# RWKV block inverse: the products Q of levels 1 to 4 as 32x32 tiles taken straight from the scores, without GpSimd's masked copy

## The reference

```python
    def step(S, inp):
        r_t, w_t, k_t, v_t, kk_t, a_t = inp
        sa = -jnp.einsum('dbhvk,dbhk->dbhv', S, kk_t)
        S = (S * w_t[..., None, :] + sa[..., :, None] * (kk_t * a_t)[..., None, :]
             + v_t[..., :, None] * k_t[..., None, :])
        return S, jnp.einsum('dbhvk,dbhk->dbhv', S, r_t)
```

## Time and profile before

| what | value |
|---|---|
| median of 3 runs | 2774.28 us (2770.97 to 2775.0) |
| the profiled execution's own time | 2774.59 us |
| its span in the profile | 2772.8 us |
| PE busy over the span | 2613.4 us, 94% |
| PEld busy | 2134.0 us, 77% |
| DVE busy | 1935.2 us, 70% |
| ACT busy | 1178.1 us, 42% |
| POOL busy | 295.0 us, 11% |
| granted clock of PE, mean | 0.979 of full |
| instructions fetched: queue q8 | 113 packets, 1.85 MB |

### The profile page before, as it was taken

How to read it: one execution, slowest core, us unless ns; L and a number is a source line. 1 busy time by engine, 2 the same in 40 slices (tenths; PEclk the granted TensorE clock), 3 DMA queues, 4 the chain that set the end, 5 groups by cost and what they waited for, 6 DMA issues and landing times. The chain is left out here.

```text
span 2772.8 us, 42554 instructions
## 1 busy us (share of the span) xinstructions
PE 2613.4 (94%) x17846; PEld 2134.0 (77%) x17846; DVE 1935.2 (70%) x1901; ACT 1178.1 (42%) x1390; POOL 295.0 (11%) x240
## 2 busy tenths in 40 slices
PE   3999978998999999999999799999999999999996
PEld 3888857776777888888888687888778888888885
DVE  5788856666576888888887878865668755555557
ACT  2555544445443333333333345555443333333332
POOL 0000001111004000000000094641040000000000
PEclk9999989998999999999999899999999999999998
DMA  8899734331548888888887366754468755555552
GB/s 310 313 330 348 288 135 132 107 126 62 213 153 297 326 304 319 310 308 322 309 320 288 116 233 241 260 167 168 155 240 324 251 187 191 190 188 193 186 195 78
DMA packets 259418, 636.55 MB, mean 230 GB/s; under 512 B 10606, under 2 KB 17444, under 8 KB 239300
## 3 DMA queue, kind: packets, MB, share of 16 engines
q1 hardware_dynamic: 253106, 621.68, 63.1%
q10 hardware_dynamic: 6162, 12.72, 1.2%
HBM read 632.25 MB, written 2.10 MB: 229 GB/s over the span
## 5 line engine op out<-in xcount | busy, mean ns | idle before, releaser
L534 DVE TENSOR_TENSOR s_wl<-s_raw,s_wh 128x2048 fp32r<-128x2048 f32 (+1 forms) x393 | 913.7, 2325 | 519.0 <-ACT s_wh L529 510.0
L529 ACT ACTIVATE s_wh<-s_raw 128x2048 fp32r<-128x2048 f32 x396 | 758.4, 1916 | 1085.2 <-PE pa L739 417.3
L737 PE MATMUL pa<-s_wh,s_hth 128*128 128x512 f32 x1312 | 527.1, 402 | 14.3 <-DVE s_wl L534 9.1
L738 PE MATMUL pa<-s_wl,s_hth 128*128 128x512 f32 x1312 | 516.9, 394 | 0.0
L739 PE MATMUL pa<-s_wh,s_htl 128*128 128x512 f32 x1312 | 516.4, 394 | 0.0
L737 PEld LDWEIGHTS pa<-s_wh,s_hth 128*128 128x128 f32 x1312 | 249.7, 190 | 76.6 <-DVE s_wl L534 13.2
L739 PEld LDWEIGHTS pa<-s_wh,s_htl 128*128 128x128 f32 x1312 | 249.8, 190 | 53.9
L738 PEld LDWEIGHTS pa<-s_wl,s_hth 128*128 128x128 f32 x1312 | 250.0, 191 | 48.8
L737 PE MATMUL pb<-s_wh,s_hth 128*128 128x512 f32 x704 | 274.1, 389 | 0.0
L738 PE MATMUL pb<-s_wl,s_hth 128*128 128x512 f32 x704 | 273.9, 389 | 0.0
L739 PE MATMUL pb<-s_wh,s_htl 128*128 128x512 f32 x704 | 273.9, 389 | 0.0
(11 more groups left out here) (406 smaller groups left out, 3446.0 us busy)
## 6 DMA issues: line engine op xcount, KB each, us to landing
s_raw<-in_ffn_w_in SPq DMA_DIRECT2D x176, 1024.0 KB, 5.3
s_adaw<-in_ada_w SPq DMA_DIRECT2D x144, 1024.0 KB, 5.4
s_raw<-in_ffn_w_out SPq DMA_DIRECT2D x88, 1024.0 KB, 7.6
s_raw<-in_ab_w_in SPq DMA_DIRECT2D x48, 1024.0 KB, 9.2
s_raw<-in_diff_w_in SPq DMA_DIRECT2D x48, 1024.0 KB, 5.2
s_adaw<-in_ada_w SPq DMA_DIRECT2D x48, 512.0 KB, 6.0
s_raw<-in_ab_w_out SPq DMA_DIRECT2D x16, 1024.0 KB, 5.2
s_qkv<-in_ada_w SPq DMA_DIRECT2D x16, 1024.0 KB, 7.2
```

Source lines behind the costliest of these rows:

```text
L529: act.activation(wh[:, s % 2, :, 0:width], raw[:, s, :, 0:width], ACT.Copy).then_inc(hi_done, 1)
L534: dve.tensor_tensor(wl[:, s % 2, :, 0:width], raw[:, s, :, 0:width], wh[:, s % 2, :, 0:width].bitcast(F32), ALU.subtract).then_inc(lo_done, 1)
L737: pe.matmul(o, a_hi, w_hi, start=start and k == 0, stop=False)
L738: pe.matmul(o, a_hi, w_lo, start=False, stop=False)
```

## The change

`level_q` takes its weights from `R_GA` itself, four 32x32 tiles a unit, as `level_v` does. `R_D`, the mask `own_block`, its 64 columns of constants, `diagonal` and the semaphore `diag_ready` are gone, with the waits on it.

```diff
-        R_D = sb("R_D", [P, NU, CH], stack=r2)
@@ POOL @@
             def own_w(t):
-                pool.wait_ge(diag_ready, t + 1)
                 pool.wait_ge(wt_ready, 4 * t + 4)
...
-            def diagonal(n):
-                pool.wait_ge(g_ready, 4 * n + 2)
-                if n:
-                    pool.wait_ge(own_ready, n)
-                    pool.wait_ge(q_done, 5 * n - 1)
-                pool.tensor_tensor(R_D[:], R_GA[:, n % 3, :, 0:CH], own_block.unsqueeze(1).to_broadcast((P, NU, CH)),
-                                   ALU.mult).then_inc(diag_ready, 1)
...
-                if t + 1 < PAIRS:
-                    diagonal(t + 1)
@@ PE, level_q @@
                     pe.wait_ge(first_ready, t + 1)
-                    pe.wait_ge(diag_ready, t + 1)
                     pe.wait_ge(wf_ready, t)
...
                 for u in range(NU):
-                    mm = two(quarter(L1Q, u), R_D[:, u], R_V[:, u], start=(u == 0))
+                    for g in range(4):
+                        r, b = slice(g * HB, (g + 1) * HB), g % 2
+                        mm = pe.matmul(quarter(L1Q, u)[r], R_GA[r, t % 3, u, b * HB:(b + 1) * HB], R_V[r, u], start=(u == 0), stop=True,
+                                       skip_group_check=True)
                 mm.then_inc(q_done, 1)
```

More of the change, by code:

```diff
@@ L67 @@
 C_FOLD = C_I2 + CH
-C_OWN = C_FOLD + P
-C_N = C_OWN + CH
+C_N = C_FOLD + P
 def constants():
@@ L104, in constants @@
     c[:, C_FOLD:C_FOLD + P] = p[:, None] % 32 == p[None, :] % 32
-    c[:, C_OWN:C_OWN + CH] = p[:, None] % CH // HB == np.arange(CH)[None, :] // HB
     return c
@@ L270, in build_trunk @@
         eye4 = cst[:, C_FOLD:C_FOLD + HB]
-        own_block = cst[:, C_OWN:C_OWN + CH]
         L1Q, L1X, L2V, C2Q = L1[:, 0:NU * HB], L1[:, W - NCH * HB:W], L2[:, 0:NU * HB], C2[:, 2 * CH:2 * CH + NCH * HB]
@@ L397, in build_trunk @@
         own_ready = sem("own_ready")
-        diag_ready = sem("diag_ready")
         wf_ready = sem("wf_ready")
```

## The result

| | median | runs |
|---|---|---|
| before | 2772.62 us | 2770.94 to 2775.0 |
| changed | 2787.31 us | 2786.01 to 2792.05 |

The ratio is 1.0053, 95% interval 1.0039 to 1.0067: the change makes the kernel 14.7 us slower. The profiled execution took 2787.97 us, 1.8 us over its span; the spans of the two profiles, 2786.2 and 2772.8 us, lie 13.4 us apart.

The account below looks back on a forecast made before the run. PE was taken to bound the RWKV stage and the projections, with stops for late instruction blocks. More blocks, +9.6 us with Q's savings included, less 1.9 for `R_V` waits gave 7.7 over 2774.6: 2782 us, range 2767 to 2793.

Parts of the forecast that it names:

- the clock's rival: RWKV stage: more stops of 2 us also lower PE's granted clock, 7 us on top, 2789 us; chance 0.13.
- What bounds the kernel: RWKV stage and projections behind it: both are PE's, so the stage's gain or loss should reach the end at full size.
- Q's burst: Q in 32 levels: 64 small entries replace 32, saving 0.18 us a level, 5.8 us less PE work (4.2 to 7.0).
- that rival (0.01): Q's burst: row tiles hinder each other when weights come from `R_GA`, 29 us in all, 2803 us; chance 0.01.
- POOL's product: DVE's L2061 falls from 1.80 to 0.54 to 0.69 us; PE's `R_V` waits in the first two pairs save 1.9 us.
- More instructions: PE in the stage: 2048 more instructions, eight blocks a step for seven, 1.2 us more a step, +9.6 us over eight.
- the time of a mean block: PE's seven other instruction blocks of a stage step: 4.0 us each, from fetching 3.5 to 4.3 us and work 3.6.
- The rival on the other side: Same block boundaries: fetching stays hidden, stops stay 9.1 us, only bursts and `R_V` count, 2767 us; chance 0.22.
- A draw: Stage steps: stops grow by about what the bursts save, 2769 to 2779 us; chance 0.22.

Follow-up runs that it names:

- nopool: The kernel before without GpSimd's product and its waits, Q still by 64x64 matmuls but from the unmasked scores (another output): 2770.87 us, ratio 0.9991.
- a_halves_now: The changed kernel with each 1 MB load for the row products issued as two halves, one right behind the other without a wait: 2786.28 us, ratio 1.0053.
- np_split4: The kernel before without GpSimd's product, Q from unmasked scores, each 1 MB load in four quarters, each issued when the one before has landed: 2805.93 us, ratio 1.0119.

## Why the prediction came out as it did

The time lies in the range, the sign was right, and so was the mechanism that gave the sign. The size was not: 7.7 us of loss were forecast and 14.7 measured. The point, 2782, missed by 5.3 us only because it was added to an execution of 2774.6 us, 2.0 us over the later median of the kernel before. By the prediction's own shares the result stands outside the forecast's 2779.8 to 2786, on the side of the clock's rival at 2789, and inside the 2780 to 2788 that it names a few lines further on.

- *What bounds the kernel.* Right. The stage's 13.9 us reach the end of the profiled execution as 13.4; the medians lie 14.7 us apart.
- *Q's burst.* Right in form: 0.68 us for 0.90, with the forecast overlap of 0.07 us at its start. With that overlap a level saves 0.74 - 0.61 = 0.13 us, the lower bound, so 32 levels save 4.2 us where 5.8 were taken. Row tiles of one bank overlap here also with the weights from `R_GA`, 64 entries of 0.2 us each in 0.68 us; that rival (0.01) did not come.
- *POOL's product.* Right in the trace: 0.69 us for 1.80. Worth 2.7 us by itself where I had 1.9; the interval holds both. I had left 0.8 us of PE's waits for `R_V`; in the changed kernel's list none of the 2.7 us is left, in nopool's 0.3.
- *More instructions.* Right in its mechanism: 121 packets, eight blocks a step, the grid of about 253. The stops, 25.6 us, came out just above the 20 to 25 forecast. Taking the loads out of the queue takes the loss out, and a pause inside the load does too.
- *The term that was mis-sized* is the time of a mean block, 4.0 us. With the 6.7 us of the long block taken off (the forecast's own figure), the steps with four loads leave (37.4 - 6.7) / 7 = 4.4 and 4.3 us, and the one with two leaves 3.8. I had 4.3 as the upper bound and took a value below it, because blocks that meet no load should be bound by work. That they meet a load by chance, and wait half of it on average, was the weak step: a load follows each row product in PE's own queue, so which fetch meets it is fixed by the program. The trace bears this out: the stops at 462.70, 534.56, 571.73 and 608.60 us, of 1.7 to 2.0 us, stand 16, 8 and 8 blocks apart, at one and the same block of their steps, and the five at another block are those named with a_halves_now.
- *The clock's rival* (0.13) came true in part, together with the forecast and not in its place. From the windows, (1 - 0.96) x 266.0 = 10.6 us of full-speed work are lost to it now, (1 - 0.97) x 252.1 = 7.6 before, so 3.1 us more, roughly, since the two shares are rounded. PE's busy time in the stage is 0.3 us more, so the bursts gave back some 3 us beside it, less than the 5.8 forecast. PE's standing time in the stage grew by 13.6 us: stops by 15.1 (24.4 us up to 650 us, before 9.3), while its other waits fell by 1.5. That the stops brought the clock down is argued: right behind the stop at 462.70 us the trace has

```profile
462.70:467.10 4.40, 4.40 (x73) 2.63 (x75) 1.77 (x4) 0.28 (x1) 0.00 (x0) 0.61 0.18 35
```

and np_split4, where PE waited most, has the lowest clock of all stages, 0.90. But behind the stop of 1.75 us at 608.60 the clock stayed at 1.00, and no run held the clock fixed.

- *The rival on the other side*, that fetching stays hidden, is refuted for the kernel as it is: 25 stops on the grid. By the Trainium skill, Runtime: NRT & Kernel Launch, Instruction fetch mechanics, PE's store holds eight blocks and crossing one is mostly hidden. The trace agrees with the 16 KB block (16.4 KB a packet) and disagrees with the rest: a late packet is followed by a stop after at most one more block, and PE goes on 2.4 us after the packet. Without loads crossing a block is nearly hidden in the kernel before (0.6 us of stops); the 7.7 us of gain that the rival forecast do not come even there, since the two kernels are then equal.
- *A draw.* Its own sums give 2768 to 2776.5 us, not the 2769 to 2779 written beside them; the measured time is outside both.

What stays open: whether the 2.4 us from packet to first use can be shortened, and how much of np_split4's lost clock comes from its waits.

## What to carry to other kernels

Where a stage runs many tiny matmuls, count PE's instructions as well as its busy time: here a block of about 253 matmuls and loads has to last some 3.5 us (an estimate: 1.1 us from call to packet and 2.4 us to first use), and a form that shortens a burst while doubling its entries can lose. Waits for "issue" that stand a whole number of blocks apart, each some 2.4 us behind a packet of the instruction queue, are late instructions, and a large load just ahead of them is the likely cause. One that does not stand so, like the 6.3 us of np_split4, is something else. A pause in that load (two halves, the second issued when the first has landed) brought back 14 us here at the price of one wait, as long as the load keeps ahead of its user.

## What the runs showed of the hardware

- An instruction packet on q8 came as the 1 MB load ahead of it in q1 ended: at 532.20 us behind a load that ran from 528.75 to 532.15. In sum, two halves back to back did the same (stops 24.2 us), two halves with a wait between them did not (14.3 us). In a_halves_now a packet also came between the two halves of a load (449.20 to 449.40 us).
- Even without the 1 MB loads, dense blocks made PE stop for 5.7 us in all, against 0.6 us with seven blocks a step.
- DVE's product of two SBUF operands took 1.80 us where POOL's product of 1.26 us began with it, 0.69 us when POOL's was gone, and 1.80 us again in the run that kept it: 1.11 us longer, most of POOL's time.
